# Moving seven weighings from the output half to the input half of a feed-forward, and taking its first two weight blocks in turn

## The reference

```python
def rms_norm(x, gain): return x * rsqrt(mean(x * x) + EPS) * gain
def swiglu(h, w_in, w_out):
    gate, up = split(h @ w_in, 2)
    return (silu(gate) * up) @ w_out
for i in range(2):                                   # first block
    sh1, sc1, g1, sh2, sc2, g2 = split(silu(c) @ w_ada[i] + b_ada[i], 6)
    x = x + g1 * mixer_i(rms_norm(x, g[i, 0]) * (1 + sc1) + sh1)
    x = x + g2 * swiglu(rms_norm(x, g[i, 1]) * (1 + sc2) + sh2, ffn_w_in[i], ffn_w_out[i])
    # the context tokens go through the same with their own condition
mod = silu(c_2) @ w_ada_2[0] + b_ada_2[0]            # second block: the last layer
...
```

## Time and profile before

| | |
|---|---|
| median of 3 runs | 1467.31 us (1466.51 to 1467.49) |
| the profiled execution | 1467.0 us, of which its span is 1465.2 us |
| PE busy | 1392.5 us, 95% |
| DVE busy | 829.4 us, 57% |
| ACT busy | 525.8 us, 36% |
| weight transfers (queue q1) | 387.72 MB |
| granted clock of TensorE, mean | 0.995 |

### The profile page before, as it was taken

The page is one execution under the profiler, slowest core; times in us unless marked ns, Lnnn a source line. Parts: engine busy times, 40 slices in busy tenths (PEclk is TensorE's granted clock), DMA queues, the critical chain, the costliest instruction groups (busy, mean ns, idle before and its releaser), DMA issues.

```text
span 1465.2 us, 20313 instructions
## 1 busy us (share of the span) xinstructions
PE 1392.5 (95%) x8088; PEld 1004.2 (69%) x8088; DVE 829.4 (57%) x1468; ACT 525.8 (36%) x1099; POOL 80.1 (5%) x74
## 2 busy tenths in 40 slices
PE   6989999999989999999999999999999999889987
PEld 3767887878867898888888999995344443334333
DVE  1878676777878867667787787774112221112113
ACT  2553222224434455455555666652111111011102
POOL 1500000000004131000000000100000000000000
PEclk9999999999999999999999999999999999999999
DMA  9947564664555322113677446369999999999995
GB/s 389 420 193 268 208 229 177 254 235 180 205 187 185 133 108 85 52 58 117 236 283 284 157 161 230 118 283 404 408 421 418 420 420 420 420 420 419 420 420 213
DMA packets 55299, 390.44 MB, mean 266 GB/s; under 512 B 6152, under 2 KB 6424, under 8 KB 9248
## 3 DMA queue, kind: packets, MB, share of 16 engines
q1 hardware_dynamic: 54608, 387.72, 66.8%
q10 hardware_dynamic: 592, 1.36, 0.3%
HBM read 388.01 MB, written 1.05 MB: 266 GB/s over the span
## 4 chain that ended last, share of the span: by engine, by line
PE 76%; DMA 16%; DVE 4%; ACT 2%; issue 1%; SPq 0%; ACTq 0%; DVEq 0%
PE twin L883 39%; DMA ring<-in_wblk 16%; PE twin L1520 12%; PE twin L969 5%; PE twin L970 3%; PE twin L927 2%; PE twin L1385 2%; PE twin L1583 1%; PE twin L809 1%; PE twin L1146 1%; PE twin L894 1%; PE twin L1505 1%; DVE wlo L2260 1%; PE twin L1210 1%; PE twin L1170 1%
## 5 line engine op out<-in xcount | busy, mean ns | idle before, releaser
L2260 DVE TENSOR_TENSOR wlo<-ring,whi 128x512 fp32r<-128x512 f32 (+1 forms) x392 | 254.2, 696 | 63.9 <-ACT whi L1697 61.2
L1697 ACT ACTIVATE whi<-ring 128x512 fp32r<-128x512 f32 (+1 forms) x392 | 216.5, 611 | 115.8 <-PE twin L883 93.2
L1520 PE MATMUL twin<-ring,xg 128*64 128x512 f32 x896 | 229.7, 596 | 13.8 <-DMA ring<-in_wblk 11.6
L883 PE MATMUL twin<-H,whi 128*128 128x512 f32 x700 | 216.4, 390 | 2.8 <-DVE H L2352 2.8
L883 PE MATMUL twin<-hsp,whi 128*128 128x512 f32 (+1 forms) x704 | 174.3, 340 | 7.5 <-DVE hsp L2451 6.5
L1520 PEld LDWEIGHTS twin<-ring,xg 128*64 128x64 f32 x896 | 72.5, 137 | 125.1 <-issue 121.4
L883 PEld LDWEIGHTS twin<-H,whi 128*128 128x128 f32 x700 | 130.9, 188 | 33.1 <-DVE H L2352 3.2
L883 PEld LDWEIGHTS twin<-hsp,whi 128*128 128x128 f32 x704 | 121.1, 191 | 24.2 <-issue 7.9
L883 PE MATMUL twin<-H,wlo 128*128 128x512 f32 x350 | 136.2, 389 | 0.0
L3013 DVE TENSOR_TENSOR rst<-rst,twin 128x512 f32<-128x512 f32 x16 | 11.0, 687 | 219.5 <-issue 213.9
L1520 PE MATMUL twin<-ring,xT 128*64 128x512 f32 x464 | 115.3, 596 | 8.8 <-DMA ring<-in_wblk 8.8
(11 more groups left out here) (410 smaller groups left out, 2404.0 us busy)
## 6 DMA issues: line engine op xcount, KB each, us to landing
ring<-in_wblk SPq DMA_DIRECT2D x325, 1024.0 KB, 12.6
front_ring<-in_wblk SPq DMA_DIRECT2D x12, 1024.0 KB, 18.8
small<-in_wblk SPq DMA_DIRECT2D x11, 1024.0 KB, 26.1
tmp<-in_wblk SPq DMA_DIRECT2D x10, 1024.0 KB, 26.5
ring<-in_wblk SPq DMA_DIRECT2D x10, 512.0 KB, 20.4
xnat<-in_xnat SPq DMA_DIRECT2D x4, 512.0 KB, 6.8
xT<-in_xin SPq DMA_DIRECT2D x1, 2048.0 KB, 21.8
tmp<-in_wblk SPq DMA_DIRECT2D x2, 512.0 KB, 20.2
```

What stands on the lines that cost most here:

```text
L883: t = e.matmul(out, a, b, start=start and n == 0, stop=stop and n == 2)
L1520: t = e.matmul(out[64 * i:64 * i + 64, :], lhs(kcs + kk, i), ws[i][:, kk, :], start=start and kk == 0, stop=stop and kk == 3)
L1697: e.activation(hi, w, ACT.Copy).then_inc(*s_hi.up(m, h))
L2260: e.tensor_tensor(lo, w, hi.bitcast(F32), ALU.subtract).then_inc(*s_lov.up(m, h))
```

## The change

It does five things. (1) All seven weighings of the last layer's set 1 get positions 1, 4, 7, 10, 13, 16 and 19 of the input half; set 0 keeps its own. With them their blocks move forward in `STREAM`. The output half has no weighing of the last layer any more. (2) PE takes the first two input blocks in turn: both for chunk 0, both for chunk 1, then in twos. ACT and DVE split block 1's first quarter ahead of the norm's first shifted chunk, and the other quarters at other chunks. (3) DVE merges a square before the join of the next chunk and not behind its addition; ACT squares at the head of a chunk. (4) PE sums the merged squares ahead of the last two rows products. (5) ACT loads the table of logarithm and exponential behind chunk 4 of the mixer and not ahead of the root.

```diff
-WEIGHED = {(0, 2 + i): (("fin", 0, 3 * i + 3), 3 * i + 2) for i in range(6)}
-WEIGHED.update({(1, 1 + i): (("fin", 0, 2 * i + 19), 2 * i + 18) for i in range(2)})
-WEIGHED.update({(1, 3 + i): (("fout", 0, j // 6, j % 6), (j, kk)) for i, (j, kk) in enumerate(((7, 0), (7, 2), (8, 0), (8, 2), (9, 1)))})
+WEIGHED = {}
+for _p in range(20):
+    if _p % 3 and _p // 3 + (_p % 3 == 1) < 8:
+        WEIGHED[(1, 1 + _p // 3) if _p % 3 == 1 else (0, 2 + _p // 3)] = (("fin", 0, _p + 1), _p)
...
-LATE_PAIRS = [(0, 0), (0, 1), (0, 2), (1, 0), (1, 1), (0, 3), (1, 2), (0, 4), (1, 3), (0, 5), (0, 6), (0, 7)] + [(1, k) for k in range(4, KC)]
+LATE_PAIRS = [(what, k) for ks in ((0,), (1,)) for k in ks for what in range(2)] + [(what, k) for a in (2, 4, 6) for what in range(2) for k in (a, a + 1)]
...
-            def sums(r):
+            def sums(r, cs=None):
                 n = NORM_N[r]
-                e.wait_ge(*s_sqm.at(r))
-                e.matmul(bank[SUM_BANK[r]][:, 0:n], ones, NORM_SQ[r][:, 0, 0:n], start=True, stop=False)
-                for c in range(MERGED[r][-1] + 1, KC - 1):
-                    e.wait_ge(*s_sqa.at(r, c))
-                    e.matmul(bank[SUM_BANK[r]][:, 0:n], ones, NORM_SQ[r][:, c, 0:n], start=False, stop=False)
-                e.wait_ge(*s_sql.at(r))
-                e.matmul(bank[SUM_BANK[r]][:, 0:n], ones, NORM_SQ[r][:, KC - 1, 0:n], start=False, stop=True).then_inc(*s_sum.up(r))
+                out, sq = bank[SUM_BANK[r]][:, 0:n], NORM_SQ[r]
+                if not cs:
+                    e.wait_ge(*s_sqm.at(r))
+                    e.matmul(out, ones, sq[:, 0, 0:n], start=True, stop=False)
+                for c in range(MERGED[r][-1] + 1, KC) if cs is None else cs:
+                    e.wait_ge(*(s_sqa.at(r, c) if c < KC - 1 else s_sql.at(r)))
+                    t = e.matmul(out, ones, sq[:, c, 0:n], start=False, stop=c == KC - 1)
+                    if c == KC - 1:
+                        t.then_inc(*s_sum.up(r))
...
+            sums(1, ())
             ada_rows(2, range(6, 8))
-            sums(1)
+            sums(1, range(MERGED[1][-1] + 1, KC))
             ada_cols(2)
             warm(3, 7)
...
             for c in range(KC):
+                if c >= 3:
+                    for a in (range(3) if c == 3 else (c - 1,)):
+                        square(1, a, lambda a: e.wait_ge(*s_fnx.at(a, 1)))
                 e.wait_ge(*s_wmm.at("fnet", c // 2, c % 2))
...
-                if c >= 2:
-                    square(1, c - 2, lambda a: e.wait_ge(*s_fnx.at(a, 1)))
-            square(1, 6, lambda a: e.wait_ge(*s_fnx.at(a, 1)))
+                if c == 4:
+                    e.preload_act_table_set(LN_EXP)
             split(20)
...
-                e.preload_act_table_set(LN_EXP)
+                if layer:
+                    e.preload_act_table_set(LN_EXP)
...
                 root(2 * layer + 1)
-                high(2 * layer + 1, {} if layer else {2: second + 2, 5: second + 4})
+                if layer == 0:
+                    split(second + 1)
+                high(2 * layer + 1, {} if layer else {3: second + 2, 5: second + 3, 6: second + 4})
...
+                    if c == 0:
+                        split(between.get("first", 0))
                     if pair and c != 1:
                         low(max(c - 1, 0))
...
             for c in range(2, KC):
+                if c >= 3:
+                    merge(1, (c - 2,))
                 join(c)
                 add_fnet(c)
-                if c >= 3:
-                    merge(1, (c - 2,))
...
-                    normed(1, between={2: second + 1, 4: second + 2, 6: second + 3})
+                    normed(1, between={"first": second + 1, 3: second + 2, 5: second + 3, 7: second + 4})
...
             def ada_fout(j, kk):
                 if j in (0, 1, 2, 3, 4, 6) and kk % 2:
                     weigh(22 + min(j, 5), kk // 2)
-                weigh_at((j, kk), (1,))
```

## The result

| | before | after |
|---|---|---|
| median | 1466.93 us (4 runs, 1466.51 to 1467.49) | 1454.26 us (4 runs, 1454.03 to 1454.49) |
| ratio, 95% interval | | 0.991 (0.9898 to 0.9923) |
| profiled execution, its span | 1467.0, 1465.2 | 1454.0, 1452.2 |
| mean granted clock of TensorE | 0.995 | 0.996 |

The change makes the kernel 12.7 us faster by the medians and 13.0 us by the profiled executions. The forecast was a gain of 11.1 us and a time of 1456.2. The measured time lies 0.3 us above the lower end of the stated range, and the gain lies above what the three parts were said to give at most (12.2 us).

A forecast was written before the change was run, and what follows sets the result against it. TensorE, busy 95% of the span, was taken as the bound, with DMA setting the pace from 1300 us on. Gains of 1.2 + 2.3 + 7.6 = 11.1 us took 1467.3 to 1456.2, range 1454.0 to 1460.0 at 75%.

The forecast's parts named there:

- the three parts: Norm's front, two blocks in turn at the feed-forward entrance, and seven moved weighings: gains of 1.2, 2.3 and 7.6 us.
- the hole: PE's 5.25 us wait near 418 us for a late load and weighing; 5.4 lost, plus 1.65 at slow clock.
- the free input half: DVE takes the moved weighings there, 89% full instead of 82%, without becoming the bound; cost 0, bounds 0 and 1.5 us.
- part 2: Feed-forward entrance: taking two blocks in turn cuts PE's waiting from 3.0 to 0.7 us, gaining 2.3; bounds 1.0 and 3.0.
- the small waits of the output half: PE's wait of 0.5 us at 454.10, behind a weighing, goes; a further 0.2 of small gaps as upper bound.
- Part 1: Ahead of the norm's root: earlier merge and sums start the columns at 85.62 instead of 86.84, gaining 1.2; bounds 0.9, 1.3.
- The table load: Moving ACT's load from ahead of the root to behind chunk 4 is worth 0.2 us at most.
- ACT's late quarter: At the entrance, ACT makes block 1's second quarter 0.6 us late, so the third low part comes at 94.9.
- The rival in which DVE sets the pace: DVE becomes the input half's bound if an operation costs 12% more; 1480 us, chance 5%.
- the gap at the entrance: Rival: the entrance only moves its gap, PE waits the old 3.0 and only 1.2 stays; 1458.5 us, chance 12%.
- no hole stayed elsewhere: Denies the rival that another load is late in the output half, leaving the hole elsewhere; 1463.3 us, chance 6%.
- the tail started as much earlier: Denies the rival that the DMA-bound tail's start does not move with PE, so no gain; 1467.3 us, chance 2%.

The follow-up runs named there:

- Run 2: Kernel after with the last layer's weighings back at their old places, so only the entrance reordered; median 1462.65 us, ratio 0.9956.
- run 1: Kernel before with only the seven weighings moved to their new positions; median 1462.49 us, ratio 0.9963.
- run 12: Kernel before with the output half's five weighings cut to 16 of 2048 columns, loads and their order kept; median 1465.42 us, ratio 0.9983.
- run 3: Kernel before with the loads of two last-layer blocks one weight block later, behind fout(0,1,2), weighings at old places; median 1467.2 us, ratio 0.9987.
- run 4: Kernel before with only the earlier merge and sums and the moved table load, blocks in the old order; median 1466.59 us, ratio 0.9989.
- run 5: Kernel after with ACT's table load put back ahead of the root; median 1454.69 us, ratio 0.9909.
- run 6: Kernel after with one unused 128x512 DVE product added at each of the 22 input-half positions; median 1455.41 us, ratio 0.9901.
- run 7: Kernel after with four unused 128x512 DVE products added at each of the 22 input-half positions; median 1466.2 us, ratio 0.9981.
- runs 9 to 11: On one chip: kernel after unchanged, 1455.96 us; kernel before unchanged, 1468.31 us; kernel after without layer 1's table load, 1453.7 us.
- before again: Kernel before, unchanged, profiled a second time on another chip; 1468.31 us in one run.

## Where the prediction held, and which of its steps failed

The mechanisms were right: the hole, the idle time at the entrance and the free input half are what the traces show. What failed is the sum. It gave 11.1 us, at most 12.2; the stages that the change touches gave 12.35, the medians 12.7. **The step that failed is the waiting that part 2 left standing, "In all 0.7 us of waiting instead of 3.0":** 0.15 us was left of more than 3.0, and the part gave 3.04 where 2.3 was forecast and 3.0 was its upper bound. The next is the 0.5 for the small waits of the output half, which gave 0.92. A third term, what comes outside the parts, was put at nothing, and the profiled execution gained 0.7 there; it is no effect of the change. That the time still fell inside the range is owed to its lower end, which was set 1.1 us below the sum of the bounds for gaps that had not been worked out and for the scatter of the runs.

**The hole** was right in place, cause and size. It is worth 7.10 us, against 5.4 and 1.65. Run 2, with the weighings at their old places, has it, run 1 has not, run 12 splits it into 3.0 us of load and 2.2 of weighing, and run 3 shows that it follows the ring's tenants. One count is wrong: the 3.48 us at the lower clock hold eight products, not nine. The 1.8 beside it, and so the 1.65, are right for eight. Two bounds do not follow from the words beside them either: 7.6 less 0.5 is 7.1 and not 6.9, and with 0.2 more it is 7.8 and not 7.9.

**The small waits** of the output half were put at 0.5 and gave 0.92. I counted the one wait that I had a row for. By the chains that place gave 0.66 (12 and 84 products with what stands between them take 28.03 us from 445.41 to 473.44 before, and 27.37 after), and 0.27 came at another, near 438.9, that I had not counted; the bound (0.2 more) was too small. Run 1 shows the whole, 8.0 for this part, against the 7.6 forecast.

**Part 1** was right: 1.29 against 1.2, and 1.26 in run 4. The first sum starts at 80.92 (forecast 81.03), the rows product ends at 83.80 (83.85), the columns start at 85.55 (85.62). The table load was put at 0.2, and run 5 gives 0.25. The sum by the drain that the Trainium skill's page "ScalarE: Activation LUTs" gives, 1.4 higher, would have been nearer to the total, but for a reason that the run refutes.

**Part 2** held in its mechanism: one more slice of products stood ready. Its working put the second low part at 92.0, PE ready at 91.8 and a wait of 0.3; on the trace the low part ends at 91.87, PE is ready at 91.77, and the wait is 0.15. The larger share is the rest of that 0.7, at the third and fourth low part. ACT's late quarter was to hold DVE back 0.6 us and did so for 0.33. The two low parts end at 94.47 and 96.05 (forecast 94.9 and 96.5), before PE wants them, at 94.79 and 96.18: PE loses nothing. So the waits left are 0.55 less than forecast. Most of the other 0.2 is a second wait of the kernel before, which the 3.0 leaves out:

```profile
96.41 0.70 PE L883 MATMUL twin<-H,whi 128*128 128x512 f32 x2
```

It starts 0.41 behind the product ahead of it and not 0.23, just behind DVE's third low part, which ends at 96.27. (The forecast's own terms put the end of the 96 products at 88.9 + 21.8 + 0.7 = 111.4, and not at 111.6.)

**The input half** cost nothing, as forecast, but the working was wrong: 89% of DVE, where the view of busy time gives 80%, and 77% by spacing. It took all weighings at 2.35 us, though it names the 1.3 of a first one itself, and added up records that overlap. The rival in which DVE sets the pace was to decide at 12% more work; in run 6 each position has one operation more, 22 x 0.69 = 15.2 us or 8% of the 184.2, for 0.55 us, and in run 7 33% more for 11.5. Where between the two it begins, no run shows.

**The other rivals** fall: the gap at the entrance went, and did not move (run 4 shows what would have been left); no hole stayed elsewhere in the change, though run 3 is that rival come true for another order of loads; the tail started as much earlier as the stages before it ended, 13.50 at 1173 us.

**Outside the parts**, 1.17 us were won up to layer 1's output half, 0.95 of it in the stretch whose length changes between profiles of one program (runs 9 to 11). That is luck, and not the change. 0.5 were lost in the tail, whose cause stays open. Of the 1.9 us by which the profiled gain of 13.0 exceeds the forecast, 1.3 are the mis-sized terms (0.74 in the pairs, 0.42 in the small waits, 0.1 in part 1), and the other 0.6 to 0.7 are these two.

## What to carry to other kernels

Where a ring is filled in order, write down for each late block which slot it takes, who lives there and what stands behind its load in the queue; take extra blocks out of the stage in which a load comes late (run 1), since a new order among the same places can just move the wait (run 3). Count an engine's load by the spacing of starts, and each kind of instruction by itself: durations of this DVE overstate it by 4% (2.35 to 2.26) to 14% (0.685 to 0.60). And let an engine that is fed too slowly work on two streams in turn: here one more slice of ready products took the place of 3 us of waiting.

## What the runs showed of the hardware that I had not expected

The wait at the entrance has two prices. In the kernels before and 1, and before again, PE waits 2.77 to 2.78 us there and the clock stays at its upper level; in runs 3 and 12 it waits the same 2.77, and then the granted clock falls to 0.50. E is 66.57 and 66.67 in these instead of 65.20 to 65.23, 1.4 us more. One microsecond of run 3, columns as in the earlier trace rows:

```profile
95.00:96.00 1.00, 1.00 (x4) 0.81 (x3) 1.00 (x4) 0.66 (x2) 0.00 (x0) 0.50 0.00 0
```

In the kernel before the same microsecond has 1.00. Up to this place the kernels before, 3 and 12 are the same but for line numbers, and both outcomes came on one chip (runs 1 and 3, runs 10 and 12). In run 4 a wait of 2.86 us left the clock at 1.00, so the length of the wait does not decide by itself. The change thus takes away a wait that costs 2.8 us in some profiles and 4.2 in others. Whether that differs between executions of one program, and how often the clock falls in runs without a profile, stays open.

The second finding is the stretch of layer 1 that takes 54.9 or 55.9 us in executions of one program, at a granted clock of 1.00. The starts of its pairs of products lie 0.347 us apart in one case and 0.353 in the other, and the spacing can change within an execution: the kernel before has 0.353 up to 742 us and 0.347 near 801, and in its second profile 0.353 in both places. What decides between them the traces don't show. It is the size of the smaller terms of this study, and only the repeats kept me from putting it down to the change.
